# Attention's softmax sums inverted once per query, on 32 partitions, with GpSimd moving them through DRAM

## The chip, the cores and the metric

The kernel runs on one core of one Trainium2 chip. The metric is the device time of one launch in microseconds (us). TensorE is called PE here, VectorE DVE, ScalarE ACT, GpSimd POOL and SyncE SP, as in the rows of the profile.

## The reference, cut to what matters

The model is two layers of a transformer block with a mixture of experts. The change is in the attention alone. It has 1024 latent tokens and 256 context tokens, and 16 heads: eight with a low-rank key and value (MLA), eight with grouped queries (GQA). Latent queries read all 1280 keys; context queries, which only layer 0 has, read the 256 context keys.

```
s = jnp.einsum('bqhgd,bkhd->bhgqk', qblk, k, preferred_element_type=jnp.float32) * scale
p = jax.nn.softmax(s, axis=-1)
return jnp.einsum('bhgqk,bkhd->bqhgd', p.astype(v.dtype), v)
...
o = jnp.concatenate([blocked_attention(qm, [kmc, km], ...), blocked_attention(qg, [kgc, kg], ...)], axis=-1)
x = layer_norm(ALPHA * x + ga * (o @ w_o[l]), ln1_g[l], ln1_b[l])
```

The softmax divides by a sum over the keys, one sum for each query and head.

## The kernel before, in words

`attention` treats the 16 heads as 8 pairs. A unit `u` is a pair of heads with some tiles of 128 queries. A latent unit has 4 tiles (512 queries) and ten steps `k`, one for each tile of 128 keys; a context unit has 2 tiles (256 queries) and two steps. Layer 0 has, for each pair, a context unit, then a latent unit (called A here), then a latent unit (B): 24 units. Layer 1 has A and B alone, 16 units, and there each latent unit follows a latent unit. Pairs 0 to 3 are MLA, with six score matmuls a step; pairs 4 to 7 are GQA, with four.

In each step PE computes the scores of this step (`scores`, L1045), ACT takes the exponential (L1108), DVE adds it into an accumulator (`accumulate`, L1169), and PE multiplies it with the values (`values`, L1059; several steps at a time at k = 2, 5 and 8, the last two in the next unit's step 0). Beside this, each step prepares a coming unit: PE computes a whole row block of its scores (`begin`, L1015) and DVE takes the maximum of each query over it (`maximum`, L1155). The function `ahead` says which: steps 0 to 5 serve the next latent unit, steps 8 and 9 the one after, steps 6 and 7 none. At step 6 the maxima are turned (L1024), copied (L1128) and written by SP as a row of the queries (L950). All `begin` calls share one PSUM area `sc`, so a `begin` waits until the maximum before it is done.

After a unit's last values, in step 0 of the next unit, ACT copies the unnormalised output to `raw` (L1115). In step 1 PE sums the accumulator over the partitions by a matmul with ones (L1069): the sums of head 0 stand alike in partitions 0 to 63, those of head 1 alike in 64 to 127. ACT copies them to `den` (L1120). DVE inverts `den` into `rinv` in pieces of `RC` = 128 queries on all 128 partitions (`invert`, L1179): four pieces in steps 6 and 7 for a latent unit, two in steps 8 and 9 for a context unit. POOL multiplies `raw` by `rinv` (L1204), and SP stores the product (L956), all in the order of the units. `raw`, `den`, `rinv` and `ot` have two buffers each.

The order of each engine's instructions is the order of the code; nothing is reordered at run time. An instruction that waits holds all that stand behind it on its engine. POOL does nothing in the attention before but the 40 multiplications.

## Time and profile before

| | us |
|---|---|
| median of 3 runs | 4173.8 (4168.7 to 4178.05) |
| the profiled execution | 4167.26 |
| its span | 4165.5 |
| attention, layer 0, from the first maxima | 463 to 1116 |
| attention, layer 1 | 2567 to 3093 |
| busy: PE, DVE, ACT, POOL | 3411.0, 2815.2, 1832.2, 1344.3 |

The span is the time from the first to the last instruction. The busy shares (PE 82%, DVE 68%) are means over stages with different limits. What the change can do is read in the two attention stages, from what PE waits for there.

### The profile page before, as it was taken

How to read it: one execution, taken by the hardware profiler on the slowest of the kernel's cores; microseconds unless marked ns; L12 is line 12 of the kernel's file. 1: busy time of each engine (PE TensorE's matmuls, PEld its weight loads, DVE VectorE, ACT ScalarE, POOL GpSimd, SP SyncE). 2: the span in 40 equal slices, each digit the busy share in tenths (PEclk: the TensorE clock that was granted, in tenths of full speed). 3: DMA queues.
4: the chain of work that ended last, by engine and by line, in shares of the span. 5: the costliest groups of instructions: out<-in, count | busy, mean ns of one | idle time of the engine just before them, and what ended most of it. 6: DMA issues, size and time to landing. Idle time of an engine off the chain costs nothing. (4 is left out here: it accounts for less than half of the span.)

```text
span 4165.5 us, 44180 instructions
## 1 busy us (share of the span) xinstructions
PE 3411.0 (82%) x14128; PEld 2192.3 (53%) x14128; DVE 2815.2 (68%) x2943; ACT 1832.2 (44%) x2102; POOL 1344.3 (32%) x889
## 2 busy tenths in 40 slices
PE   5999598888588599999938994999868589999960
PEld 2554354544244488888814442554424368888850
DVE  1444366776455699899846663777854578989966
ACT  0222232333200388888823331333320068888850
POOL 2111000000100387777732210000010077777750
PEclk9999699998798699999969996999989789999985
DMA  7554621110222499688743326111022159797953
GB/s 291 198 204 158 160 50 45 44 33 24 107 87 89 193 396 355 265 317 321 305 181 120 125 95 176 47 50 41 16 93 86 67 234 383 307 361 298 354 226 115
DMA packets 247658, 730.56 MB, mean 175 GB/s; under 512 B 49232, under 2 KB 137072, under 8 KB 194184
## 3 DMA queue, kind: packets, MB, share of 16 engines
q0 software_dynamic: 104272, 508.74, 31.5%
q1 hardware_dynamic: 130328, 174.51, 13.6%
q10 hardware_dynamic: 12960, 46.15, 3.2%
q8 instruction: 44, 0.72, 0.1%
q14 instruction: 54, 0.44, 0.0%
HBM read 715.09 MB, written 129.34 MB: 203 GB/s over the span
## 5 line engine op out<-in xcount | busy, mean ns | idle before, releaser
L1879 DVE TENSOR_TENSOR ex_wl<-ex_wr,ex_wh 128x2048 fp32r<-128x2048 f32 x440 | 988.0, 2288 | 61.7 <-ACT ex_wh L1824 61.7
L1824 ACT ACTIVATE ex_wh<-ex_wr 128x2048 fp32r<-128x2048 f32 x440 | 842.7, 1915 | 73.7 <-PE ex_yp L1787 53.5
L1108 ACT ACTIVATE at_pt<-at_st 128x1024 f32<-128x1024 f32 (+1 forms) x336 | 336.6, 1004 | 652.4 <-PE at_st L1045 651.4
L1155 DVE TENSOR_REDUCE at_nm<-at_sc 128x1 f32<-128x1280 f32 (+1 forms) x276 | 376.7, 1365 | 254.6 <-PE at_sc L1015 252.3
L715 PE MATMUL zp<-w_in,hT 128*128 128x480 f32 x960 | 428.5, 580 | 24.8 <-ACT z L378 23.2
L1204 POOL TENSOR_TENSOR at_ot<-at_raw,at_rinv 128x512 f32<-128x512 f32 (+1 forms) x40 | 49.9, 1248 | 1229.7 <-DVE at_rinv L1179 1229.7
L1169 DVE TENSOR_TENSOR at_acc<-at_acc,at_pt 128x1024 f32<-128x1024 f32 x256 | 312.8, 1222 | 103.5 <-ACT at_pt L1108 102.2
L1367 PE MATMUL mr_mp<-mr_w_o,mr_oT 128*128 128x512 f32 x576 | 283.5, 655 | 100.8 <-DVE mr_bc L1435 40.9
L1059 PE MATMUL at_op<-at_pt,at_va 128*64 128x512 f32 (+1 forms) x1344 | 331.1, 623 | 0.2
L1705 POOL DMA_INDIRECT ex_wr<-in_w_down,piece_of x152 | 314.3, 2068 | 46.3 <-issue 46.3
L1045 PE MATMUL at_st<-at_q,at_km 96*128 96x512 f32 (+3 forms) x1008 | 272.4, 411 | 34.8 <-DMA at_q<-at_nmT 34.8
L715 PEld LDWEIGHTS zp<-w_in,hT 128*128 128x128 f32 x960 | 173.4, 194 | 172.8 <-issue 145.5
L1045 PEld LDWEIGHTS at_st<-at_q,at_km 96*128 96x128 f32 (+1 forms) x1008 | 183.8, 197 | 137.7 <-issue 55.3
L1367 PEld LDWEIGHTS mr_mp<-mr_w_o,mr_oT 128*128 128x128 f32 x576 | 119.6, 211 | 254.8 <-issue 190.8
L1764 PE MATMUL ex_gp<-ex_wh,ex_xh 128*128 128x512 f32 x576 | 226.7, 394 | 13.4 <-DVE ex_wl L1879 13.4
L1705 POOL DMA_INDIRECT ex_wr<-in_w_gate,piece_of x152 | 222.6, 1465 | 46.4 <-issue 46.4
L1782 PE MATMUL ex_yp<-ex_wh,ex_hh 128*128 128x512 f32 x576 | 233.2, 405 | 0.0
L1725 POOL DMA_INDIRECT y_s<-ex_y,row_to x72 | 193.0, 2680 | 118.6 <-ACT ex_y L1832 117.4
L1783 PE MATMUL ex_yp<-ex_wl,ex_hh 128*128 128x512 f32 x576 | 227.6, 395 | 0.0
L1765 PE MATMUL ex_gp<-ex_wl,ex_xh 128*128 128x512 f32 x576 | 226.1, 393 | 0.0
L1766 PE MATMUL ex_gp<-ex_wh,ex_xl 128*128 128x512 f32 x576 | 225.8, 392 | 0.0
L1766 PE MATMUL ex_vp<-ex_wh,ex_xl 128*128 128x512 f32 x576 | 224.5, 390 | 0.0
(266 smaller groups left out, 6003.9 us busy)
## 6 DMA issues: line engine op xcount, KB each, us to landing
ad_w<-in_w_ada POOLq DMA_DIRECT2D x48, 1024.0 KB, 10.6
q_mla<-qT SPq DMA_DIRECT2D x40, 384.0 KB, 3.9
k_mla<-kT SPq DMA_DIRECT2D x40, 384.0 KB, 5.8
at_km<-k_mla SPq DMA_DIRECT2D x16, 960.0 KB, 12.3
at_q<-q_mla SPq DMA_DIRECT2D x32, 384.0 KB, 12.6
w_in<-in_w_in SPq DMA_DIRECT2D x2, 5760.0 KB, 32.5
q_gqa<-gqT SPq DMA_DIRECT2D x20, 512.0 KB, 6.7
cy<-y_s POOLq DMA_DIRECT2D x10, 1024.0 KB, 5.2
```

What stands on the lines that cost most here:

```text
L715: ins = nc.tensor.matmul(zp[:, n, 0:ZW], hT[:, k, :], w_in[:, k, n * ZW:(n + 1) * ZW], start=(k == 0), stop=(k == KC - 1))
L1045: ins = nc.tensor.matmul(st[:, j % 2, h, 0:nq], kk, qq, start=(m == 0), stop=(m == len(passes) - 1))
L1059: ins = nc.tensor.matmul(op[VD * h:VD * h + VD, 0:nq], va[:, k, col * VD:(col + 1) * VD], pt[:, j % PT, h, 0:nq], start=(k == 0), stop=(k ...
L1108: nc.scalar.activation(pt[:, j % PT, :, 0:nq], st[:, j % 2, :, 0:nq], ACT.Exp).then_inc(exp_done, 1)
L1155: nc.vector.tensor_reduce(nm[:, v % 3, s:s + 1], score_bank(A_NO[v, s])[:, 0:kb * P], AX.X, ALU.max, negate=True).then_inc(max_done, 1)
L1169: nc.vector.tensor_tensor(out, before, pt[:, j % PT, :, 0:nq], ALU.add).then_inc(acc_done, 1)
L1367: ins = nc.tensor.matmul(mp[:, n * 512:(n + 1) * 512], oT[:, k, :], w_o[:, k, n * 512:(n + 1) * 512], start=(k == 0), stop=(k == KC - 1))
L1705: pool.indirect_dma_start(wr[:, u, p].rearrange("p a n -> p (a n)"), None, w, bass.IndirectOffsetOnAxis(R["wi"][:, p % 2, b:b + 1], 0), bo ...
L1766: ins = nc.tensor.matmul(out[:, :], xl[:, k, :], wh[:, q, j, :], start=False, stop=(k == KC - 1))
L1782: nc.tensor.matmul(out, hh[:, 2 * k + c, :], W[0][:, c, cols], start=(k == 0 and c == 0), stop=False)
L1824: nc.scalar.activation(wh[:, q], wr[:, u, p], ACT.Copy).then_inc(hi_done, 1)
L1879: nc.vector.tensor_tensor(wl[:, q], wr[:, u, p], wh[:, q].bitcast(F32), ALU.subtract).then_inc(lo_done, 1)
```

## The change

`RC` becomes 32. DVE no longer inverts the sums on 128 partitions, where 64 partitions hold the same numbers. POOL takes one row of each head (the rows that differ) from `den` to a DRAM buffer `den_s`, and from there to a tile `dc` in which 1024 sums stand as 32 partitions of 32 (512 sums as 16 of 32). DVE inverts that into `rc` in one instruction. POOL writes `rc` to DRAM (`inv_s`) and reads each head's inverses back into 64 partitions of `rinv`. Each transfer is waited for before the next that reads it. POOL does this for one unit after the other, and the unit's multiplication stands at the end of its chain. `inverted` says where DVE's instruction stands: after a latent unit in step 5, after a context unit in step 2 for the unit before it and in step 8 for the context unit itself. The last unit of a layer is not moved: DVE inverts its sums from PSUM in one instruction of 512 columns and multiplies itself; ACT's copy of them goes.

```diff
-    PT, QR, RC = 8, 5, P
+    PT, QR, RC = 8, 5, 32
+    def inverted(u, k):
+        if U[u][3] != NT or u == 0:
+            return []
+        if U[u - 1][3] == NT:
+            return [u - 1] if k == 5 else []
+        return [u - 2] if k == 2 and u > 1 else [u - 1] if k == 8 else []
...
-            take_sums(len(U) - 1)
...
-            def invert(u, pieces):
-                for i in pieces:
-                    if i == 0:
-                        dve.wait_ge(den_taken, u + 1)
-                        if u > 1:
-                            dve.wait_ge(ot_ready, u - 1)
-                    part = slice(i * RC, (i + 1) * RC)
-                    nc.vector.reciprocal(rinv[:, u % 2, part], den[:, u % 2, part]).then_inc(inv_done, 1)
+            def invert(u):
+                dve.wait_ge(dc_loaded, 16 * (u + 1))
+                n = 2 * U[u][2] * P // RC
+                nc.vector.reciprocal(rc[0:n, u % 2, :], dc[0:n, u % 2, :]).then_inc(inv_done, 1)
...
-                    if k in (6, 7):
-                        w = u - 2 if u and U[u - 1][3] != NT else u - 1
-                        if w >= 0:
-                            invert(w, range(2 * (k - 6), 2 * (k - 5)))
-                    if k in (8, 9) and u and U[u - 1][3] != NT:
-                        invert(u - 1, [k - 8])
-            invert(len(U) - 1, range(4))
+                    for w in inverted(u, k):
+                        invert(w)
+            u = len(U) - 1
+            nq = U[u][2] * P
+            dve.wait_ge(r_full, u + 1)
+            dve.wait_ge(ot_ready, u - 1)
+            nc.vector.reciprocal(rinv[:, u % 2, 0:nq], op[:, 0:nq]).then_inc(inv_done, 1)
+            dve.wait_ge(inv_done, u + 1)
+            dve.wait_ge(op_taken, u + 1)
+            dve.wait_ge(o_stored[u % 2], 16 * (u // 2))
+            dve.wait_ge(ot_ready, u)
+            nc.vector.tensor_tensor(ot[:, u % 2, ...], raw[:, u % 2, 0:nq], rinv[:, u % 2, 0:nq], ALU.mult)...
...
-            for u in range(len(U)):
-                nq = U[u][2] * P
-                pool.wait_ge(inv_done, pieces_done(u))
+            for u in range(len(U) - 1):
+                nq, s = U[u][2] * P, u % 2
+                n = 2 * nq // RC
+                pool.wait_ge(den_taken, u + 1)
+                for h in range(2):
+                    pool.dma_start(S["den_s"][s:s + 1, h * nq:(h + 1) * nq], den[VD * h:VD * h + 1, s, 0:nq])...
+                pool.wait_ge(den_kept, 32 * (u + 1))
+                pool.dma_start(dc[0:n, s, :], S["den_s"][s, 0:2 * nq].rearrange("(p b) -> p b", b=RC))...
+                pool.wait_ge(inv_done, u + 1)
+                pool.dma_start(S["inv_s"][s, 0:2 * nq].rearrange("(p b) -> p b", b=RC), rc[0:n, s, :])...
+                pool.wait_ge(r_kept, 16 * (u + 1))
+                if u >= 2:
+                    pool.wait_ge(ot_ready, u - 1)
+                for h in range(2):
+                    pool.dma_start(rinv[VD * h:VD * h + VD, s, 0:nq], S["inv_s"][s, h * nq:(h + 1) * nq].partition_broadcast(VD))...
+                pool.wait_ge(r_spread, 32 * (u + 1))
```

DVE, layer 0, from step 5 of unit A of the second pair to the context unit behind it, before (`at_nm` are the maxima, `at_acc` the accumulators, `at_den` the sums on 128 partitions):

```order
L1169 TENSOR_TENSOR at_acc<-at_acc,at_pt 128x1024 x2
L1179 RECIPROCAL at_rinv<-at_den 128x128 x2
L1169 TENSOR_TENSOR at_acc<-at_acc,at_pt 128x1024
L1179 RECIPROCAL at_rinv<-at_den 128x128 x2
L1155 TENSOR_REDUCE at_nm<-at_sc 128x1
L1169 TENSOR_TENSOR at_acc<-at_acc,at_pt 128x1024
L1179 RECIPROCAL at_rinv<-at_den 128x128
L1155 TENSOR_REDUCE at_nm<-at_sc 128x1
L1169 TENSOR_TENSOR at_acc<-at_acc,at_pt 128x1024
L1179 RECIPROCAL at_rinv<-at_den 128x128
```

The same engine and place in the changed kernel, from step 2 of that unit on (`at_dc` are the sums as 32 or 16 partitions of 32):

```order
L1175 TENSOR_TENSOR at_acc<-at_acc,at_pt 128x1024
L1181 RECIPROCAL at_rc<-at_dc 32x32
L1161 TENSOR_REDUCE at_nm<-at_sc 128x1
L1175 TENSOR_TENSOR at_acc<-at_acc,at_pt 128x1024
L1161 TENSOR_REDUCE at_nm<-at_sc 128x1
L1175 TENSOR_TENSOR at_acc<-at_acc,at_pt 128x1024
L1161 TENSOR_REDUCE at_nm<-at_sc 128x1
L1175 TENSOR_TENSOR at_acc<-at_acc,at_pt 128x1024 x3
L1161 TENSOR_REDUCE at_nm<-at_sc 128x1
L1175 TENSOR_TENSOR at_acc<-at_acc,at_pt 128x1024
L1181 RECIPROCAL at_rc<-at_dc 16x32
L1161 TENSOR_REDUCE at_nm<-at_sc 128x1
```

The four large inversions no longer stand between step 6 and the maximum of step 8; a small one stands behind step 2 and another behind step 8.

POOL, layer 0, a latent unit and the context unit behind it, before:

```order
L1204 TENSOR_TENSOR at_ot<-at_raw,at_rinv 128x512 x2
L1204 TENSOR_TENSOR at_ot<-at_raw,at_rinv 128x256
L1204 TENSOR_TENSOR at_ot<-at_raw,at_rinv 128x512 x2
L1204 TENSOR_TENSOR at_ot<-at_raw,at_rinv 128x256
L1204 TENSOR_TENSOR at_ot<-at_raw,at_rinv 128x512 x2
```

POOL in the changed kernel, one latent unit and the context unit behind it (`den_s` and `inv_s` are in DRAM):

```order
L1212 DMA den_s<-at_den 16x1x32 x2
L1214 DMA at_dc<-den_s 32x32
L1216 DMA inv_s<-at_rc 32x32
L1221 DMA at_rinv<-inv_s 64x512 x2
L1225 TENSOR_TENSOR at_ot<-at_raw,at_rinv 128x512
L1212 DMA den_s<-at_den 16x1x16 x2
L1214 DMA at_dc<-den_s 16x32
L1216 DMA inv_s<-at_rc 16x32
L1221 DMA at_rinv<-inv_s 64x256 x2
L1225 TENSOR_TENSOR at_ot<-at_raw,at_rinv 128x256
```

Each multiplication now has six transfers ahead of it, and the context unit's sums leave `den` only when the unit before it is multiplied.

## Rows read from the trace of the kernel before

**Rows 1.** Windows of the two attention stages: stretch, length, busy, clock, DMA.
```profile
463.00:1116.00 653.00, 536.72 (x2120) 295.46 (x2120) 436.63 (x392) 203.76 (x249) 35.02 (x36) 0.89 0.20 52
2567.00:3093.00 526.00, 465.55 (x1878) 252.61 (x1876) 391.65 (x328) 184.27 (x207) 21.76 (x16) 0.95 0.17 41
```

**Rows 2.** Waits of PE in these stretches: total us, times, longest.
```profile
PE at_sc L1015 <- DVE at_nm L1155: 68.1, 64, 1.8
...
PE at_sc L1015 <- DVE at_nm L1155: 30.6, 57, 1.4
```

**Rows 3.** Timeline of DVE, layer 1, GQA: start, us, instruction.
```profile
2901.30 1.76 DVE L1179 RECIPROCAL at_rinv<-at_den 128x128 f32<-128x128 f32 x2
...
2905.72 1.43 DVE L1155 TENSOR_REDUCE at_nm<-at_sc 128x1 f32<-128x1280 f32 x1
```

**Rows 4.** Timeline of PE: idle before and its releaser, in brackets.
```profile
698.26 0.84 PE L1015 MATMUL at_sc<-at_km,at_q 96*128 96x512 f32 x3 [1.10 <-DVE at_nm L1155]
...
917.30 0.84 PE L1015 MATMUL at_sc<-at_kg,at_q 128*128 128x512 f32 x3 [1.36 <-DVE at_nm L1155]
...
920.63 0.84 PE L1015 MATMUL at_sc<-at_kg,at_q 128*128 128x512 f32 x3 [1.54 <-DVE at_nm L1155]
...
2779.40 0.85 PE L1015 MATMUL at_sc<-at_km,at_q 96*128 96x512 f32 x3 [0.33 <-DVE at_nm L1155]
...
2907.20 0.86 PE L1015 MATMUL at_sc<-at_kg,at_q 128*128 128x512 f32 x3 [1.39 <-DVE at_nm L1155]
...
2922.08 0.85 PE L1015 MATMUL at_sc<-at_kg,at_q 128*128 128x512 f32 x3 [0.66 <-DVE at_nm L1155]
```

**Rows 5.** Groups of instructions, DVE, line 1179: count, busy, mean ns, idle before.
```profile
L1179 DVE RECIPROCAL at_rinv<-at_den 128x128 f32<-128x128 f32 x144 | 127.2, 922 | 3.6 <-ACT at_den L1120 3.6
```

**Rows 6.** Timeline, ACT's copies of sums, and DVE behind steps 2 and 5.
```profile
889.92 0.60 ACT L1120 ACTIVATE at_den<-at_op 128x512 f32<-128x512 f32 x1 [0.59 <-PE at_op L1069]
...
900.38 1.49 DVE L1155 TENSOR_REDUCE at_nm<-at_sc 128x1 f32<-128x1280 f32 x1 [0.87 <-PE at_sc L1015]
...
2915.24 0.60 ACT L1120 ACTIVATE at_den<-at_op 128x512 f32<-128x512 f32 x1 [0.58 <-PE at_op L1069]
...
2930.41 1.22 DVE L1169 TENSOR_TENSOR at_acc<-at_acc,at_pt 128x1024 f32<-128x1024 f32 x1 [2.18 <-ACT at_pt L1108]
```

**Rows 7.** Timeline of PE, last score matmul of step 9, unit A, GQA.
```profile
915.54 0.40 PE L1045 MATMUL at_st<-at_q,at_kl 65*128 65x512 f32 x1
```

**Rows 8.** Transfers by line: engine, count, KB each, median us from issue to landing.
```profile
cy<-y_s POOLq DMA_DIRECT2D x10, 1024.0 KB, 5.2
...
o_s<-at_ot SPq DMA_DIRECT2D x32, 256.0 KB, 2.5
...
mod<-ada POOLq DMA_DIRECT2D x4, 4.0 KB, 8.1
```

**Rows 9.** Line 1705, POOL's gathers of weights: issue to landing.
```profile
DMA to landing us min/median/max: 2.1/10.1/18.6
```

**Rows 10.** Line 1306, POOL: ns min/median/max of issuing a small transfer.
```profile
L1306 POOL DMA_DIRECT2D mr_b_r<-in_b_router_exp x2: 547/547/547, 1114.6 to 3102.2; - x2
```

**Rows 11.** DMA busy tenths in 40 slices of 886 to 926.
```profile
DMA  4999699200000000000000000000000071000047
```

**Rows 12.** Timeline, end of layer 1's attention; line 1401, a product of 128x512.
```profile
3087.92 0.60 ACT L1120 ACTIVATE at_den<-at_op 128x512 f32<-128x512 f32 x1 [2.20 <-PE at_op L1069]
3088.55 3.39 DVE L1179 RECIPROCAL at_rinv<-at_den 128x128 f32<-128x128 f32 x4 [1.81 <-ACT at_den L1120]
3092.02 1.26 POOL L1204 TENSOR_TENSOR at_ot<-at_raw,at_rinv 128x512 f32<-128x512 f32 x1 [6.36 <-DVE at_rinv L1179]
...
L1401 DVE TENSOR_TENSOR mr_u<-mr_mp,mr_bc x36: 680/692/693, 1149.0 to 3286.6; 128x512 f32<-128x512 f32 x36
```

**Rows 13.** Windows of two units of layer 1, GQA.
```profile
2905.88:2936.13 30.25, 26.70 (x109) 13.83 (x109) 24.99 (x22) 11.45 (x13) 1.26 (x1) 1.00 0.13 35
2936.13:2969.26 33.13, 29.54 (x109) 14.93 (x109) 25.08 (x22) 11.47 (x14) 1.26 (x1) 0.90 0.12 33
```

More of the change, by code:

```diff
@@ L897, in attention @@
         rinv = sb("rinv", [P, 2, 512])
+        dc = sb("dc", [2 * 512 // RC, 2, RC])
+        rc = sb("rc", [2 * 512 // RC, 2, RC])
         ot = sb("ot", [P, 2, 4, P])
@@ L908, in attention @@
         v_done, acc_done, op_taken = sem("v_done"), sem("acc_done"), sem("op_taken")
+        den_kept, dc_loaded, r_kept, r_spread = sem("den_kept"), sem("dc_loaded"), sem("r_kept"), sem("r_spread")
         r_full, den_taken, inv_done, ot_ready, o_stored = sem("r_full"), sem("den_taken"), sem("inv_done"), sem("ot_ready"), [sem(f"o_stored{s}") for s in range(2)]
@@ L914, in score_bank @@
             return st[:, :, :, :].rearrange("p b h n -> p (b h n)") if n < PRO and n % 2 else sc
-        def pieces_done(u):
-            return sum(unit[2] * P // RC for unit in U[:u + 1])
         def sums_done(u):
@@ new lines, in _ @@
+            nq = U[u][2] * P
[6 more added lines that the diff above has]
+            dve.wait_ge(ot_ready, u)
+            nc.vector.tensor_tensor(ot[:, u % 2, 0:U[u][2], :].rearrange("p a n -> p (a n)"), raw[:, u % 2, 0:nq],
+                                    rinv[:, u % 2, 0:nq], ALU.mult).then_inc(ot_ready, 1)
@@ L2018, in backbone @@
     dram("y_s", [NT * P * TOPK, D])
+    dram("den_s", [2, 2 * 512])
+    dram("inv_s", [2, 2 * 512])
     with ExitStack() as cx:
```

10 lines of the change are left out of this document (7 added, 3 removed).

## The prediction, made before the changed kernel ran

> **What bounds the kernel now.** I read the windows of the two attention stages first. They last 653 and 526 us, and PE is busy for 536.7 and 465.6 of them [rows 1], so PE is the engine to follow there: time that it does not wait is time won, as long as nothing else becomes late. The waits of PE come next. Its largest wait that recurs is that of the score block for a coming unit (L1015) for the maximum before it: 68.1 us in layer 0 and 30.6 us in layer 1 [rows 2]. That is the most that any relief of DVE could give back, 98.7 us; the question is which of these waits have an inversion ahead of them. The timelines of DVE and PE side by side tell. In a GQA unit of layer 1 two inversions stand behind step 6 and two behind step 7, and the maximum of step 8 starts only at 2905.72 [rows 3], though its scores were there some 4 us earlier; it ends at 2907.15, and PE, which has waited 1.39 us, starts the next block at 2907.20 [rows 4]. Where no inversion is near (steps 4 and 5), PE still waits 0.66 us [rows 4]: the step's four score matmuls are shorter than a maximum. That floor stays.
>
> **What goes.** DVE's 144 inversions of 128x128 take 127.2 us, 922 ns each [rows 5]. In their place stand 38 of 32 columns or fewer and two of 512. If the price goes by the columns (4 x 128 columns take 3.39 us in the end stage [rows 12], 6.6 ns a column), the small one costs 0.21 us, with a start of some tenths at most 0.4; 38 of them are 8 to 15 us of DVE. All of that has idle time of DVE behind it: 0.87 us after step 2 and 2.18 us after step 5 [rows 6]. I take its cost on the path as nothing; without that cover it would be at most 0.4 x 38 = 15 us. So DVE loses about 110 us of work, but little of it was on the path. By kind of unit (a wait and its floor; the row shown stands for its kind):
> - layer 1, GQA, B or A: the wait at step 9 is 1.36 to 1.39 in six units, 8.2 us in all; it goes. The wait one block later (0.75) falls to 0.66: 0.5 in all.
> - layer 1, MLA: 0.31 to 0.35 at step 9 in seven units, 2.3 us, goes; one block later 0.28 falls to 0.17 in six: 0.7.
> - layer 0, GQA, unit A, where the context unit's two inversions stand too: 1.36 and 1.54 us [rows 4], of which 0.66 stays: 2.25 each in three units, 6.7 us. The last pair has nothing to prepare.
> - layer 0, MLA, unit A: 0.33 and 1.10 [rows 4], of which 0.2 stays, three units: 3.7 us.
> - layer 0, GQA, unit B: 0.2 us, three times: 0.6. The waits of 1.6 to 1.8 us in these units, two blocks in a row with one maximum between, stay; they are most of layer 0's 68.1.
>
> Sum: 8.2 + 0.5 + 2.3 + 0.7 = 11.7 in layer 1 and 6.7 + 3.7 + 0.6 = 11.0 in layer 0.
>
> **The last unit.** Before: ACT's copy starts at 3087.92, the four inversions at 3088.55 take 3.39, POOL's product starts at 3092.02 and takes 1.26, end 3093.28 [rows 12]. After: DVE starts where ACT did, 3.4 us for 512 columns, then a product of 128x512 at 0.69 [rows 12]: 3087.92 + 3.4 + 0.07 + 0.69 = 3092.1. That is 1.2 us in each layer, 2.4 together, if POOL has finished the unit before it (below).
>
> **What comes in: 228 transfers on POOL's queue.** Six for each of 38 units. POOL itself is idle, and an issue costs it 0.55 us [rows 10]. What counts is the chain. Let H be the time from issue to landing of one. Sums to `dc`: 0.55 + 2H (two issues, a landing, a load). Inverses to `rinv` and the product: 2H + 0.55 + 1.27. No such transfer stands in this trace. From below: POOL's gathers landed in 2.1 us at best [rows 9]. From above: POOL's 4 KB ones in 8.1 us, in pieces of single numbers [rows 8]. Between: a store of 256 KB from SBUF to DRAM 2.5 us, and 1 MB by POOL 5.2 us [rows 8]. The nearest rows are the store and the fastest gather, so I take H = 2.3. Then `dc` is ready 5.2 us after the sums and the product ends 6.4 us after the inversion.
>
> The Trainium skill ("DMA: Bandwidth & Descriptors", section "Anatomy of one DMA") gives a transfer of this kind a fixed cost of about 2.0 us; by it the two chains would be 4.6 and 5.8 us, and the sum the same. No row here shows so small a transfer of POOL's alone.
>
> The windows these have to fit:
> - Step 5, layer 1: sums at 2915.24 + 0.60 = 2915.84, DVE needed again at 2930.41 [rows 6]: 14.6 us against 5.2. Free until H = 7.0.
> - Step 2, layer 0, GQA (the narrowest): sums at 890.52, DVE needed at 900.38 [rows 6]: 9.9 us against 5.2. Free until H = 4.6. The DMA engines are nine tenths busy up to 893 with query loads [rows 11], so H may be 1 or 2 us more for the first hop.
> - Step 8, layer 0: the context unit's sums can leave only after the unit before is multiplied. From the inversion at step 2 (about 899.6) POOL needs 2H + 1.8, then 0.55 + 2H: 4H + 2.4 = 11.6 us. DVE is needed for the maximum of step 9, whose block follows the scores of step 9 (last one at 915.54 + 0.28) by 0.75: about 916.6 [rows 7]. 17.0 us against 11.6. Free until H = 3.6. This is the tightest place.
> - Last unit: its steps are short, about 8.5 us from the sums to step 5 and 2.3 idle, 10.8 against 5.2; the product of the unit before ends about 9 us ahead of the end.
>
> SP waits for a product a little later or earlier than now, and its next loads are four units ahead of use. `raw` of a unit is overwritten two units later. Both are covered by more than 10 us.
>
> **Sum.** 11.0 + 11.7 + 2.4 = 25.1 us off the profiled execution's 4167.3: 4142. That execution was 6.5 us below the median of the runs shown, so in terms of that median 4173.8 - 25 = 4149.
>
> **Rivals.**
> 1. The clock pays too. Of two like units one took 30.25 us at a granted clock of 1.00 and the next 33.13 at 0.90 [rows 13]: stretches of 1.2 GHz cost 2.9 us there. Over layer 1 from step to step four such dips cost 6.7 us, in layer 0's GQA pairs and one MLA pair about 11. If fewer and shorter waits of PE kept the clock up, all of it might come on top: 25 + 14 = 39, 4135. For it: a dip followed waits. Against: the units before had the same waits and no dip, and the long waits of layer 0's B units stay.
> 2. The gain is eaten. Transfers under load take 4 to 4.5 us: step 8 is then late by 4 x 4.3 + 2.4 - 17.0 = 2.6 us in seven A units, 18 us, or the waits removed at step 9 return at the next block. About 4168.
> 3. Slower: the chain on POOL at step 8. Above H = 3.6 each further us of H costs 4 us in each of the seven A units of layer 0, because DVE stands still there with maxima behind it and PE behind those. Gain and loss balance at 25 / 28 = 0.9 more, H = 4.5; at H = 6 step 8 would be 9.4 us late and, with step 2 late by 2.7 already, the loss is 7 x 9.4 = 66 us, the time 4173.8 + 41 = 4215. For it: the 8.1 us row and the load at 886 to 893 [rows 8, 11]. Against: the engines are nearly idle for 17 of the 24 us after, and that row's 1024 pieces of 4 bytes are not like these 32 pieces of 128.
>
> The Trainium skill (the same page, "Latency and other measured facts") gives DRAM access 0.2 us on average and 2 us at high load. With 2 us more on the one hop that falls into the busy stretch, step 2 would need 7.2 of 9.9 us, and the sum stays; the rule counts against the change only if the load lasts, and [rows 11] show it ending at 893.
>
> 4. The change could miss its aim if the maximum of step 8 waited for something else. Its scores end some 4 us before it starts, and DVE is busy without a gap in between, so I give it nothing of its own.
>
> **Chances.** Forecast 0.62 (its own range 4141 to 4157), rival 1 0.14, rival 2 0.14, rival 3 0.10. What this kernel's measurement can tell from no change is about 0.2%, 8 us. Faster by more than that: the forecast, rival 1 and a fifth of rival 2, 0.77; within: 0.13; slower: 0.10. The range that should hold 8 in 10 is 4136 to 4170: the lower end cuts half of rival 1, the upper takes in rival 2 and leaves out rival 3.
>
> **What would show it.** Right: at step 9 PE's wait for L1155's line is gone in layer 1 and its GQA units take about 28.8 us instead of 30.25; DVE's small inversions take 0.2 to 0.4 us and DVE waits for no transfer ahead of them; the waits of 1.6 to 1.8 us in layer 0's B units are unchanged; after the sums the load of `dc` lands within 6 us; the end of the stage is a DVE product. Wrong: DVE idle ahead of the inversion at step 8 or 2 with a DMA as releaser (rival 3 or 2); waits at step 9 gone but as much added at the block after (rival 2); unit times shorter than 28.8 with a clock of 1.00 throughout (rival 1).

## The result and the profile after

| | median of n runs, us | kernel before in the same call | ratio, 95% interval |
|---|---|---|---|
| the changed kernel | 4127.56 (4121.3 to 4130.12), 4 | 4171.25, 4 | 0.9890 (0.9871 to 0.9908) |
| its profiled execution | 4127.45 | 4167.26 | |

The change took 43.7 us off by the medians and 39.9 us by the two profiled spans. The forecast was 25, which gave 4149 by the median that the prediction started from, with 4136 as the lower end of the range: the direction was right, the gain was forecast too small. Of the runs below, one execution of f4_idle_inv took 4876.61 us at a granted clock of 0.713; its times are read from the other three.

The two attention stages of the changed kernel, in the same columns as [rows 1]:

```profile
465.00:1092.00 627.00, 532.39 (x2120) 294.90 (x2120) 386.05 (x337) 203.16 (x248) 98.35 (x161) 0.90 0.23 59
2535.00:3053.00 518.00, 470.20 (x1904) 258.42 (x1903) 366.26 (x289) 183.97 (x207) 68.47 (x105) 0.95 0.22 59
```

DVE (the third of the busy times) is busy for 50.6 us less in layer 0. POOL (the fifth) went from 35.0 to 98.4 us there, for the issues. What PE waited for, in the changed kernel, first layer 0 and then layer 1, answers to [rows 2]:

```profile
PE at_sc L1022 <- DVE at_nm L1161: 58.5, 55, 1.9
...
PE at_sc L1022 <- DVE at_nm L1161: 18.7, 48, 0.8
```

9.6 us less in layer 0 and 11.9 us less in layer 1 (there the longest wait is now 0.8 us, not 1.4). Together 21.5 us: about half of the 39.9. The rest has to be found elsewhere. I cut both spans at ACT's copies to `raw`, of which each unit has one:

| us | before | after | less |
|---|---|---|---|
| start to the first copy | 504.3 | 507.1 | -2.7 |
| layer 0, units | 591.8 | 578.6 | 13.2 |
| its end (last copy to last product) | 8.1 | 5.9 | 2.2 |
| between the attention stages | 1520.2 | 1514.7 | 5.5 |
| layer 1, MLA units 1 to 7 | 224.4 | 219.6 | 4.8 |
| layer 1, GQA units 8 to 13 | 188.2 | 172.7 | 15.5 |
| layer 1, the last two units | 48.1 | 48.1 | 0.0 |
| its end | 8.2 | 5.9 | 2.2 |
| after it | 1072.2 | 1073.0 | -0.8 |

Of DVE in a GQA unit of layer 1 the timeline of the changed kernel reads as follows, where [rows 3] had two inversions of 1.76 us together and a late maximum:

```profile
2897.45 1.22 DVE L1175 TENSOR_TENSOR at_acc<-at_acc,at_pt 128x1024 f32<-128x1024 f32 x1
2898.58 0.33 DVE L1181 RECIPROCAL at_rc<-at_dc 32x32 f32<-32x32 f32 x1
2900.85 2.56 DVE L1175 TENSOR_TENSOR at_acc<-at_acc,at_pt 128x1024 f32<-128x1024 f32 x2 [1.93 <-ACT at_pt L1115]
2903.32 1.48 DVE L1161 TENSOR_REDUCE at_nm<-at_sc 128x1 f32<-128x1280 f32 x1
```

The small inversion costs 0.33 us and DVE is idle for 1.93 us behind it: it is hidden. The maximum of step 8 starts with no idle time and ends at 2904.80, ahead of PE, which starts the block of step 9 without a wait at 2906.37 and waits only at the block after it (timeline of PE, the changed kernel; the bracket is the idle time before):

```profile
2906.37 0.75 PE L1022 MATMUL at_sc<-at_kg,at_q 128*128 128x512 f32 x3
2907.14 0.50 PE L1052 MATMUL at_st<-at_q,at_kg 128*128 128x512 f32 x1
2907.48 0.39 PE L1052 MATMUL at_st<-at_q,at_kl 65*128 65x512 f32 x1
...
2908.70 0.85 PE L1022 MATMUL at_sc<-at_kg,at_q 128*128 128x512 f32 x3 [0.36 <-DVE at_nm L1161]
```

The chain on POOL for the same unit, each row with what POOL waited for:

```profile
2886.57 1.02 POOL L1212 DMA_DIRECT2D den_s<-at_den  x2 [9.14 <-ACT at_den L1127]
2888.93 0.51 POOL L1214 DMA_DIRECT2D at_dc<-den_s  x1 [1.33 <-DMA den_s<-at_den]
2899.21 0.51 POOL L1216 DMA_DIRECT2D inv_s<-at_rc  x1 [9.77 <-DVE at_rc L1181]
2901.08 1.04 POOL L1221 DMA_DIRECT2D at_rinv<-inv_s  x2 [1.37 <-DMA inv_s<-at_rc]
2904.73 2.35 POOL L1225 TENSOR_TENSOR at_ot<-at_raw,at_rinv 128x512 f32<-128x512 f32 x1 [2.61 <-DMA at_rinv<-inv_s]
```

A hop of this chain takes 1.6 or 1.7 us from issue to landing at the median (2.9 for the one that spreads a row over 64 partitions), and the sums are in `dc` some 4 us after the first issue. DVE waited for `dc` twice in the whole kernel:

```profile
DVE at_rc L1181 <- DMA at_dc<-den_s: 4.6, 2, 2.4
```

### The profile page after: what moved, and what is told of

It reads as the page before. It is cut to its first block and busy times, and to the rows that moved or that the text cites. A ratio compares the mean times of both kernels' runs of the same rounds, so it can differ in the third digit from the quotient of the medians.

```text
span 4125.6 us, 44304 instructions
## 1 busy us (share of the span) xinstructions
PE 3399.1 (82%) x14128; PEld 2189.6 (53%) x14128; DVE 2727.7 (66%) x2841; ACT 1830.7 (44%) x2100; POOL 1459.5 (35%) x1115
## 5 line engine op out<-in xcount | busy, mean ns | idle before, releaser
L1175 DVE TENSOR_TENSOR at_acc<-at_acc,at_pt 128x1024 f32<-128x1024 f32 x256 | 321.7, 1257 | 120.7 <-ACT at_pt L1115 118.5
L1785 PE MATMUL ex_vp<-ex_wh,ex_xh 128*128 128x512 f32 x576 | 224.1, 389 | 0.0
```

The source lines that it names most:

```text
L1175: nc.vector.tensor_tensor(out, before, pt[:, j % PT, :, 0:nq], ALU.add).then_inc(acc_done, 1)
L1785: nc.tensor.matmul(out[:, :], xh[:, k, :], wh[:, q, j, :], start=(k == 0), stop=False)
```

## The experiments

Twelve runs were made: of nine new kernels, and once more of the kernel before, of the changed one and of e3_xfer. In the comparison, "clean" means a unit that took its shortest time, in which TensorE was granted 2.4 GHz throughout; "half clock" is the time at 1.2 GHz in the clock record of the trace, counted from the span's start as the windows are. The table has the values on which the verdicts rest, in us. GQA and MLA are clean units of layer 1; "six" is the time of its GQA units 8 to 13 together. The runs were made in several calls, and the kernel before had medians from 4167.57 to 4181.37 in them, so whole times of different rows are compared by their ratios, each of which is against the kernel before in its own call.

| kernel | median | ratio, interval | layer 0 units, half clock | MLA | GQA | six, half clock |
|---|---|---|---|---|---|---|
| before (first profile) | 4171.25 | | 591.8, 89 | 32.05 | 30.24 | 188.2, 17 |
| f1_before2 | 4178.3 | 1.0005 (0.9983 to 1.0027) | 605.8, 126 | 32.05 | 30.24 | 183.4, 10 |
| e3_xfer | 4181.73 | 1.0025 (1.0007 to 1.0043) | 595.1, 96 | 32.05 | 30.24 | 185.9, 14 |
| f2_xfer2 | 4173.34 | 0.9991 (0.9971 to 1.0011) | 585.8, 70 | 32.05 | 30.25 | 184.7, 17 |
| f3_swap_before | 4136.87 | 0.9910 (0.9879 to 0.9941) | 562.8, 55 | 32.06 | 30.19 | 187.2, 14 |
| f4_idle_inv | 4130.7 | 0.9913 (0.9881 to 0.9945) | 571.6, 61 | 31.36 | 30.23 | 185.7, 14 |
| e2_moved | 4162.57 | 0.9972 (0.9955 to 0.9989) | 599.8, 102 | 31.36 | 29.05 | 174.3, 0 |
| e1_small | 4137.85 | 0.9911 (0.9881 to 0.9941) | 568.8, 58 | 31.35 | 28.52 | 172.8, 3 |
| after | 4127.56 | 0.9890 (0.9871 to 0.9908) | 578.6, 82 | 31.36 | 28.52 | 172.7, 3 |
| e4_after2 | 4127.47 | 0.9892 (0.9861 to 0.9923) | 572.6, 68 | 31.35 | 28.53 | 171.2, 0 |
| e6_noend | 4129.71 | 0.9907 (0.9876 to 0.9938) | 574.8, 72 | 31.36 | 28.52 | 172.8, 3 |
| e5_long | 4189.29 | 1.0045 (1.0023 to 1.0067) | 643.1, 147 | 31.4 | 28.5 | 173.6, 3 |
| e7_swap | 4097.62 | 0.9827 (0.9790 to 0.9864) | 547.8, 36 | 31.36 | 28.50 | 171.0, 0 |
| e8_mix | 4095.91 | 0.9831 (0.9794 to 0.9867) | 545.7, 44 | 31.36 | 28.52 | 171.2, 0 |

The first five rows have the long wait at step 9 of layer 1's GQA units by nature, the sixth has it put back, the other eight don't have it. The expectations below count the half clock by windows that lie 10.6 us too early in the clock record: where they say 97, 14, 7 to 14 and 0 to 3 us for rows of this table, it is 89, 17, 10 to 17 and 0 to 3, and their 324 between the attention stages is 320.

### e1_small: the DVE time of the inversions alone

```diff
                     part = slice(i * RC, (i + 1) * RC)
+                    part = slice(i * RC, i * RC + 8)
...
-                                        rinv[:, u % 2, 0:nq], ALU.mult).then_inc(ot_ready, 1)
+                                        den[:, u % 2, 0:nq], ALU.mult).then_inc(ot_ready, 1)
```

> The kernel before with each inversion cut from 128 to 8 columns and left in its place; POOL multiplies by the sums. Left out: 15 of 16 inversions, so the output is not the softmax's. Theory (only DVE's time ahead of the maximum of step 8 counts, and a wait of PE costs its idle time plus about 0.26 us of restart): units of layer 1 take 31.4 us (MLA) and 28.5 us (GQA), GQA unit A of layer 0 28.2 us, as in the changed kernel, and the whole some 40 us less than before, 4131 or a few less since no unit waits for a transfer and the end has no long inversion. Rival (the gain needs the new places of the instruction or the free ACT copy): units of 32.05 and 30.25 us stay, time within 10 us of before. Rival (only the idle time in the rows counts): gain of at most 30 us.

Measured: 4137.85 us. The attention has no transfer here and its layer 1 units are as short as in the changed kernel (31.35 and 28.52 us). So the gain inside the units is the DVE time taken off, and the transfers give nothing of it back there. The end stages are shorter (4.2 us each), which is the four inversions cut to 8 columns, and the stages behind the second attention take 1088 us in place of 1073. Since the values differ, the routing of the experts does too, so the whole time says nothing; only the units are read.

### e2_moved: the place alone

`inverted` is the changed kernel's.

```diff
-                    if k in (6, 7):
-                        w = u - 2 if u and U[u - 1][3] != NT else u - 1
-                        if w >= 0:
-                            invert(w, range(2 * (k - 6), 2 * (k - 5)))
-                    if k in (8, 9) and u and U[u - 1][3] != NT:
-                        invert(u - 1, [k - 8])
+                    for w in inverted(u, k):
+                        invert(w, range(U[w][2]))
```

> The kernel before with its 128x128 inversions, all of them, moved to the places of the changed kernel (step 5, or steps 2 and 8 after a context unit), no transfers. Theory: behind step 5 there are 2.2 us idle and slack up to the maximum of step 8, so layer 1 gains nearly all (units 31.4 and 28.5 us); behind step 2 there is only 0.9 us idle for 3.4 us of work, so GQA unit A of layer 0 takes about 31 us, no better than 30.7 before. Whole: about 4153. Rival (the amount of DVE work alone counts): no change, 4171. Rival (place alone counts): 4131 as in the changed kernel.

Measured: 4162.57 us. The full-size inversions at the new places are enough for MLA in layer 1 (31.36 us, all of the gain) and for two thirds of it in GQA. The timeline of PE around step 9 in this kernel shows why a third is missing:

```profile
2899.92 0.84 PE L1023 MATMUL at_sc<-at_kg,at_q 128*128 128x512 f32 x3 [0.17 <-DVE at_nm L1163]
2902.45 0.84 PE L1023 MATMUL at_sc<-at_kg,at_q 128*128 128x512 f32 x3 [0.74 <-DVE at_nm L1163]
```

The long wait fell to 0.17, but the next stayed at 0.74. In layer 0 four inversions do not fit behind step 2: in each of its A units with grouped queries PE waited 2.94 us there, and two of the three waited for maxima as long in all as before (4.35 and 4.42 us against 4.3); with 7 us of half clock in each they took 32.7 to 33.7 us. The layer's 8 us more than the first profile of before are within what two profiles of that kernel differ by. So the place gives most of layer 1's gain, and in layer 0 it gives none without the size: in e1_small, with the size alone, the A units with grouped queries took 28.20 to 28.23 us, as in the changed kernel. The whole time, 4162.57 us, lies some 10 us above the 4153 expected.

### e3_xfer and f2_xfer2: the transfers alone

The same kernel ran in two calls:

```diff
+                if u < len(U) - 1:
+                    n = 2 * nq // 32
+                    pool.wait_ge(den_taken, u + 1)
+                    for h in range(2):
+                        pool.dma_start(S["den_s"][s:s + 1, h * nq:(h + 1) * nq], den[VD * h:VD * h + 1, s, 0:nq])...
...
                 pool.wait_ge(inv_done, pieces_done(u))
+                if u < len(U) - 1:
+                    pool.dma_start(S["inv_s"][s, 0:2 * nq].rearrange("(p b) -> p b", b=32), dc[0:n, s, :])...
...
+                    for h in range(2):
+                        pool.dma_start(spread[VD * h:VD * h + VD, s, 0:nq], S["inv_s"][s, h * nq:(h + 1) * nq].partition_broadcast(VD))...
```

> The kernel before with POOL's six transfers a unit added, whose result nobody uses; DVE inverts on 128 partitions as before. Theory (transfers are hidden): units of 32.05, 30.25 and 30.7 us as before, time within 8 us of before, 4171. Rival (228 transfers cost through shared DMA engines or queues): slower by 10 us or more, with PE waits for at_q or at_km.

> The kernel before with all of the changed kernel's small transfers added, unused; the same as the run before of this kind. Theory (the transfers cost next to nothing in the attention and the 10 us of the medians were real but lie elsewhere, in how the experts' stages fall): a ratio of 1.002 to 1.003 again, units of 32.05 and 30.24 us at full clock as in the kernel before. Rival (the 10 us were scatter): a ratio of 0.999 to 1.001. A second rival (the transfers slow the attention's own steps): units longer than those of the kernel before by 0.2 us or more at full clock.

Measured: 1.0025 the first time and 0.9991 the second, with units of 32.05 and 30.24 us at full clock both times. The 228 transfers cost the attention nothing that can be seen. Behind the second attention both profiles took longer, 1079.4 and 1080.0 us against 1072.2 and 1073.5 in the two of the kernel before; e6_noend has 1078.3 too, and no run tells whether the transfers have a part in it. The 10 us of the first run did not come again: the interval of the first run leaves 1.000 out, that of the second holds it. A difference of this size had better be repeated before it is explained.

### e4_after2: the changed kernel again

> The changed kernel once more, for its time beside the others on one chip and for a second sample of the clock. Theory (some 5 us of the gain is the clock, which varies from run to run): about 4128 to 4135, unit times without a dip again 31.4, 28.5 and 28.2 us, dips in other places. Rival (the clock's part is fixed by the change): again a single dip in layer 1 between 2600 us and the stage's end.

Measured: 4127.47 us against 4127.56. In this profile no unit of layer 1 has a stretch of half clock.

### e5_long: a longer chain on POOL

```diff
+                for i in range(HOPS):
+                    pool.dma_start(dx[0:n, s, :], S["den_s"][s, 0:2 * nq].rearrange("(p b) -> p b", b=RC))...
+                    pool.wait_ge(x_loaded, 16 * (HOPS * u + i + 1))
```

(`HOPS` is 4; the loop stands ahead of the load of `dc`.)

> The changed kernel with four more loads, one after the other, ahead of each load of the 32 partitions: the sums reach DVE 4 x 1.9 = 7.5 us later. Theory: the windows are real. Layer 1 has 14.6 us and needs 4.4 + 7.5 = 12, so its units stay 31.4 and 28.5 us. In layer 0 DVE stands still behind step 2 for about 5 us in GQA unit A, and about 2 us behind step 8: some 50 us more than the changed kernel, 4178, which is slower than the kernel before. Rival (DVE's waits there are made up later): under 15 us more than the changed kernel. Rival (a hop costs PE everywhere): layer 1 slows as well.

Measured: 4189.29 us, some 60 above the changed kernel (59.6 above e6_noend in the same call) and 1.0045 of the one before. Layer 1's units did not change. In layer 0 DVE stood still, in order of time (timeline of DVE, this kernel):

```profile
859.01 0.34 DVE L1184 RECIPROCAL at_rc<-at_dc 32x32 f32<-32x32 f32 x1 [5.71 <-DMA at_dc<-den_s]
879.63 0.34 DVE L1184 RECIPROCAL at_rc<-at_dc 16x32 f32<-16x32 f32 x1 [4.65 <-DMA at_dc<-den_s]
```

and PE's waits for maxima went from 58.5 to 101.3 us, half clock in layer 0's units from 82 to 147. So the rival that ended slower is a real mechanism, at the places that the prediction named (steps 2 and 8 of the A units of layer 0); with hops of 1.6 to 2.9 us at the median the changed kernel is on the safe side of it.

### e6_noend: the end as before

```diff
-            dve.wait_ge(r_full, u + 1)
+            dve.wait_ge(den_taken, u + 1)
...
-            nc.vector.reciprocal(rinv[:, u % 2, 0:nq], op[:, 0:nq]).then_inc(inv_done, 1)
...
-            nc.vector.tensor_tensor(ot[:, u % 2, 0:U[u][2], :]...
+            for i in range(4):
+                part = slice(i * P, (i + 1) * P)
+                nc.vector.reciprocal(rinv[:, u % 2, part], den[:, u % 2, part]).then_inc(inv_done, 1)
...
+            nc.gpsimd.tensor_tensor(ot[:, u % 2, 0:4, :]...
```

> The changed kernel with the last unit of each layer as before: ACT copies the sums, DVE inverts four pieces, POOL multiplies. Theory (the end gained 2.2 us a layer, of which 1.0 is that DVE no longer has inversions ahead of its last additions): from ACT's copy of the values to the end 7.1 us instead of 5.9 (and 8.1 before), so 2.4 us more in all; by the total not to be told from the changed kernel, 4130. Rival (all 2.2 us are the shorter end): 8.1 us as before.

Measured: the segment from the last copy to the last product takes 7.22 us here, 5.94 in the changed kernel and 8.12 to 8.16 before. The shorter path of the last unit is worth 1.28 us a layer, as forecast (1.2). Another 0.9 us a layer comes from something else, told below.

### e7_swap, e8_mix and f3_swap_before: the waits that stayed

In layer 0's B units the score blocks of the coming latent and context unit stand in turn, and PE waits 1.6 to 1.8 us at several of them. e7_swap puts the context block first and takes both maxima into one turn:

```diff
-            return [(LATENT[n + 1], k + 2)] + ([(u + 1, k - 2)] if k >= 2 and U[u + 1][3] == CT else [])
+            return ([(u + 1, k - 2)] if k >= 2 and U[u + 1][3] == CT else []) + [(LATENT[n + 1], k + 2)]
...
-                pe.wait_ge(max_done, A_NO[v, 2 * na - 1] + 1)
+                w = v + 1 if v and U[v][3] == CT else v
+                pe.wait_ge(max_done, A_NO[w, 2 * U[w][2] - 1] + 1)
```

e8_mix has the second edit too, and moves two of the four context blocks into step 7 of the A unit:

```diff
+            return ([(u + 1, k - 2)] if k >= 4 and U[u + 1][3] == CT else []) + [(LATENT[n + 1], k + 2)]
+        if k == 7 and u + 2 < len(U) and U[u + 2][3] == CT:
+            return [(u + 2, 0), (u + 2, 1)]
```

> The changed kernel with the order of the two score blocks turned in layer 0's B units: the context unit's small block (maximum 0.42 us) first, the latent unit's (1.49 us) second; the turn waits for both maxima. Theory (long waits of PE for a maximum cost their time and pull the clock down): the four waits of 1.6 to 1.8 us a unit become about 0.6 us, B units are 4 us shorter in 7 pairs, and fewer dips of the clock follow: 28 to 40 us less than the changed kernel, about 4095. Rival (the waits move to the next block, behind the latent maximum): no gain beyond 8 us, since the next step's first block then waits for that maximum.

> As the swapped one, but two of the context unit's four blocks are made in step 7 of unit A, which is free since no inversion stands there any more. Theory: only two double steps are left in B units; gain over the changed kernel 28 to 40 us, some us more than the swap alone if step 7 has room. Rival (step 7 of unit A is full): A units grow by what B units lose.

f3_swap_before is the edit of e7_swap on the kernel before, inversions and all.

> The kernel before, with its large inversions left, and the order of two maxima changed: in layer 0's B units the score block of the coming context unit goes ahead of the latent one, and the wait of the step covers both maxima. In the changed kernel this took about 30 us off. Theory (this gain needs nothing of the inversions, it lies in steps 2 to 7 of the B units, where DVE has room in both kernels): 4171 - 30 = 4141, a ratio of 0.993, layer 0's units from 592 to about 562 us. Rival (it needs the DVE time that the inversions take, because in the kernel before two of them stand in each of the steps 6 and 7): half of it or less, 4155 to 4165, a ratio of 0.996 to 0.998, and the waits of PE at steps 7 to 9 of the B units grow from 0.7 to 1.5 us or more.

Measured: 4097.62, 4095.91 and 4136.87 us. The two orders cannot be told apart by their times: in e8_mix the A units with grouped queries grew from 28.2 to 29.9 and 31.4 us, and the B units behind them shrank from 34.3 to 34.9 us down to 32.3, so that the rival of that run describes it better than its theory. The swap takes 32 us off e6_noend in the same call, and by the ratio 38 us (25 to 51) off the kernel before: it needs nothing of the change. The two gains add within the noise: 0.9890 x 0.9910 is 0.980, and 0.9827 (0.9790 to 0.9864) was measured. The windows of layer 0's units, first of the changed kernel, then of e7_swap, tell how much of it is clock:

```profile
507.05:1085.65 578.60, 508.70 (x2051) 279.58 (x2051) 364.26 (x320) 198.52 (x241) 98.35 (x161) 0.93 0.17 46
```

```profile
505.41:1053.19 547.78, 496.98 (x2051) 271.35 (x2051) 361.02 (x319) 198.40 (x241) 98.20 (x161) 0.97 0.18 48
```

Half clock fell from 82 to 36 us. The same 2051 matmuls are busy for 11.7 us less, at a mean clock of 0.97 instead of 0.93; PE's waits for maxima fall from 58.5 to 39.2, 19.3 us. Their sum, 31.0, is the gain of the stretch (30.8).

### f1_before2 and f4_idle_inv: does the wait at step 9 pull the clock down?

f1_before2 is the kernel before, unchanged. f4_idle_inv is the changed kernel with the DVE work of before put back in layer 1's GQA units, its result unused:

```diff
+                    if len(U) == 16 and 8 <= u <= 14 and k in (6, 7):
+                        for i in range(2 * (k - 6), 2 * (k - 5)):
+                            nc.vector.reciprocal(spare[:, i * P:(i + 1) * P], den[:, (u - 1) % 2, i * P:(i + 1) * P])
```

> The kernel before, unchanged, once more, for its clock. Both theories expect the same time, 4165 to 4178 us, and the same waits at full clock: 1.36 to 1.39 us at step 9 of the units with grouped queries in layer 1, units of 30.2 us. They part on the half clock (1.2 GHz) in the six units 8 to 13 of layer 1. Theory (the long waits at step 9 let the clock fall): again some 14 us of half clock there, at least 8, and over 100 us in layer 0's units and the stages between taken as 97 and 324. Rival (the dips fall where they fall, and before and the kernel with added transfers were unlucky): 0 to 3 us as in the eight kernels without those waits.

> The changed kernel with four unused inversions of 128x128 put back behind steps 6 and 7 of the units with grouped queries of layer 1 (units 8 to 14), where the kernel before had its own; nothing else. All theories expect the wait at step 9 to come back at 1.36 to 1.39 us. Theory (a wait of PE costs its idle time and some 0.26 us of restart, and waits of this length let the clock fall): units 8 to 13 at full clock 30.24 us again instead of 28.52, and half clock of 7 to 14 us in them instead of 0 to 3; 171.1 + 6 x 1.72 + 3 to 7 = 184 to 188 us for the six, the whole kernel about 4127 + 13 = 4140. Rival A (a removed wait is worth its idle time alone, 1.45 us with the block after): 29.97 us, 180 to 181 us for the six. Rival B (the clock there has nothing to do with this wait): 30.24 us a unit but half clock of 0 to 3 us, 181 to 183 us for the six.

Measured in f4_idle_inv: the wait is back, and so are the unit of 30.23 us and the half clock, 14 us in the six units. The whole time does not show it: 4130.7 us where 4140 was expected, against 4127.5 for the changed kernel in other calls, by ratios that overlap. PE's wait, timeline of this kernel:

```profile
2912.34 0.84 PE L1023 MATMUL at_sc<-at_kg,at_q 128*128 128x512 f32 x3 [1.38 <-DVE at_nm L1162]
2914.86 0.84 PE L1023 MATMUL at_sc<-at_kg,at_q 128*128 128x512 f32 x3 [0.75 <-DVE at_nm L1162]
```

The windows of the six units, one fence each for before, after and f4_idle_inv (the last three numbers are clock, DMA share and GB/s):

```profile
2848.84:3037.01 188.17, 167.42 (x655) 86.14 (x656) 150.37 (x126) 68.84 (x79) 7.58 (x6) 0.95 0.08 22
```

```profile
2825.89:2998.60 172.71, 161.52 (x655) 83.97 (x656) 136.57 (x108) 68.87 (x78) 28.26 (x42) 0.99 0.12 33
```

```profile
2823.94:3009.59 185.65, 165.49 (x655) 85.79 (x656) 151.80 (x132) 68.80 (x78) 26.19 (x42) 0.96 0.11 31
```

655 matmuls each, with a clock of 0.95, 0.99 and 0.96. Over fourteen profiles the half clock of these units is 17, 10, 14, 17, 14 and 14 us in the six with the wait and 0, 3, 3, 0, 3, 3, 0 and 0 in the eight without it, in the order of the table: no overlap. The places of the dips say the same. The six profiles have 21 of them in these units, and 20 begin 0.2 to 2.8 us after the start of a block that had waited 1.36 to 1.39 us. One of them, behind the block that started at 2972.8 in f4_idle_inv, with the stretch after it (windows, the clock is the third number from the end):

```profile
2973.40:2976.70 3.30, 3.30 (x9) 1.99 (x7) 3.02 (x3) 1.02 (x1) 0.00 (x0) 0.50 0.00 0
2976.80:2980.20 3.40, 3.40 (x15) 1.65 (x15) 1.49 (x1) 0.95 (x2) 0.00 (x0) 1.00 0.00 0
```

The other rival would be that DVE's inversions bring the dips by themselves and not through PE's wait. e2_moved speaks against it: there DVE does the same work in these units (154.9 us busy, 150.4 before), the wait at step 9 is 0.17 us, and the clock never falls:

```profile
2847.00:3021.30 174.30, 160.01 (x657) 83.00 (x655) 154.94 (x126) 68.87 (x78) 12.73 (x6) 1.00 0.09 23
```

So the rival that the dips fall by chance is out; that a wait there brings them is shown by taking it away and by putting it back, the latter in one profile. How strongly they come is a matter of chance all the same: f1_before2 had 10 us where the first profile had 17 (its expectation asked for at least 8 in its own count, by which it is 7). And it is not the only thing that brings them: of the four dips in the eight profiles without the wait, three stand behind a wait of 0.75 us in step 5 and one behind a wait of 1.60 us for a row of maxima.

The other half of that expectation holds too: the units are 30.23 us, not the 29.97 of the rival that counts idle time alone. Where the 0.26 us lie is read from start to start, in the row above and in the changed kernel's rows ahead of the experiments. With the wait the two blocks start 2.52 us apart (2912.34, 2914.86), without it 2.33 (2906.37, 2908.70): 0.2 less, where the forecast had 0.09 (0.75 to 0.66). And counted from ACT's copy to `raw`, the first block starts 24.94 us into the unit with the wait and 23.43 without it, 1.5 us for a bracket of 1.38. The rows are from a clean unit of f4_idle_inv and from the changed kernel, where 2906.37 stands above:

```profile
2917.62 0.60 ACT L1123 ACTIVATE at_raw<-at_op 128x512 f32<-128x512 f32 x1 [2.45 <-PE at_op L1067]
2942.56 0.84 PE L1023 MATMUL at_sc<-at_kg,at_q 128*128 128x512 f32 x3 [1.38 <-DVE at_nm L1162]
```

```profile
2882.94 0.60 ACT L1122 ACTIVATE at_raw<-at_op 128x512 f32<-128x512 f32 x1 [2.11 <-PE at_op L1066]
```

## Why the prediction was wrong in size

Point by point, in the order of its working:

- **PE is the engine to follow, its waits for maxima the prize.** Right. In each clean unit the time follows PE's waits. The waits of 1.6 to 1.8 us in the B units stayed, as forecast.
- **The waits of layer 1.** Forecast 11.7 us, measured 6 x 1.73 + 7 x 0.69 = 15.2. Every wait went that was to go. One step failed here: taking a wait's price from its bracket, and the next one's floor from a bracket elsewhere. In GQA the two parts are 1.5 and 0.2 us, where the brackets had 1.36 and 0.09. The floor of 0.66 was itself well read: at step 4 of a unit of the changed kernel the blocks are 2.33 us apart, as they now are at step 9.

```profile
2861.66 0.75 PE L1022 MATMUL at_sc<-at_kg,at_q 128*128 128x512 f32 x3
...
2863.99 0.85 PE L1022 MATMUL at_sc<-at_kg,at_q 128*128 128x512 f32 x3 [0.66 <-DVE at_nm L1161]
```

  But at step 9 the same 2.33 us show a bracket of 0.36, since PE's first matmul behind the block starts 0.77 us after it there and takes 0.50, against 0.58 and 0.39 at step 4, and 2.52 us show 0.75. A bracket depends on how fast PE ran ahead of it; the distance between two starts does not. In MLA it is the same, 0.69 us against 0.44 by brackets (timeline of PE, first before, then the changed kernel):

```profile
2681.24 1.68 PE L1045 MATMUL at_st<-at_q,at_km 97*128 97x512 f32 x6
2683.24 0.85 PE L1015 MATMUL at_sc<-at_km,at_q 96*128 96x512 f32 x3 [0.33 <-DVE at_nm L1155]
2683.93 1.57 PE L1045 MATMUL at_st<-at_q,at_km 97*128 97x512 f32 x6
```

```profile
2662.44 1.67 PE L1052 MATMUL at_st<-at_q,at_km 97*128 97x512 f32 x6
2663.95 0.74 PE L1022 MATMUL at_sc<-at_km,at_q 96*128 96x512 f32 x3
2664.52 1.57 PE L1052 MATMUL at_st<-at_q,at_km 97*128 97x512 f32 x6
```

  From the matmuls ahead of the block to those behind it it is 2683.93 - 2681.24 = 2.69 us with a wait of 0.33 and 2.08 without: 0.61 us. The block itself takes 0.11 us longer after a wait, and it starts 0.16 later than the bracket alone explains.
- **The waits of layer 0.** Forecast 11.0. By the brackets A units gave 2.55 (GQA, three) and 1.22 (MLA, three), with the small ones of the B units 11.8 us, but two units kept a wait that was to go, 2.2 us (next point): 9.6, what the sums of PE's waits show. The MLA units gave 0.27 each on top (the one that kept no wait went from 32.44 to 30.96 us, 1.48 for 1.22), but the GQA units gave just their brackets (30.74 to 28.20, 2.54 for 2.55); no run tells why they differ. Right in size.
- **The small inversion, 0.2 to 0.4 us, hidden.** Right: 332 to 341 ns, 38 times, and the 16x32 ones took as long as the 32x32 ones.
- **Transfers: H = 2.3 and free below 3.6.** Right as a bound, with one exception. The first chain took some 4 us where 5.2 were forecast; the second, from DVE's inversion to the end of the product, took 7.0 to 8.2 where 6.4 were, for the spread takes 2.9 us and the product up to 2.35. First hops beside loads took 4.4 to 4.6 us in layer 0's GQA units and up to 6.1 in layer 1, within the windows. In layer 0's second and third A unit the first hop fell into the load of the next keys and queries:

```profile
666.06 1.03 POOL L1212 DMA_DIRECT2D den_s<-at_den  x2 [11.87 <-ACT at_den L1127]
675.64 0.51 POOL L1214 DMA_DIRECT2D at_dc<-den_s  x1 [8.55 <-DMA den_s<-at_den]
678.94 0.51 POOL L1216 DMA_DIRECT2D inv_s<-at_rc  x1 [2.80 <-DVE at_rc L1181]
```

  The second of its two transfers landed 8.8 us after its issue, DVE stood still for 2.43 us and PE for 1.39 instead of 0.17. The prediction had looked at the DMA load of one GQA unit only [rows 11]. The Trainium skill ("DMA: Bandwidth & Descriptors", section "Latency and other measured facts") gives 2 us of DRAM access at high load; the 8.8 us here are 7 above an undisturbed hop, and the measurement decides. For an undisturbed hop the same page's 2.0 us (section "Anatomy of one DMA") stands against 1.6 or 1.7 here.
- **The last unit.** Forecast 1.2 us a layer, measured 2.2. The edit itself gave 1.28 (e6_noend). The other 0.9 is a collision that the prediction had not seen. Timelines of the kernel before, of POOL, DVE and PE:

```profile
3083.54 2.12 POOL L1204 TENSOR_TENSOR at_ot<-at_raw,at_rinv 128x512 f32<-128x512 f32 x1 [20.78 <-DVE at_rinv L1179]
...
3083.38 3.36 DVE L1169 TENSOR_TENSOR at_acc<-at_acc,at_pt 128x1024 f32<-128x1024 f32 x2
...
3086.80 1.08 PE L1069 MATMUL at_op<-at_acc,c_ones 128*64 128x512 f32 x4 [1.72 <-DVE at_acc L1169]
```

  POOL's product of the last unit but one takes 2.12 us instead of 1.26, DVE's two additions beside it 3.36 instead of 2.49, and PE's sums wait 1.72 us for them. In e3_xfer and f2_xfer2 the product comes some microseconds later, the additions take 2.49 and the end is 7.24 to 7.29 us with all four inversions in it: 0.9 less, without the edit. In the changed kernel the product is over in time and PE's sums wait 0.79 us, for ACT. The Trainium skill ("SBUF — State Buffer", section "Who interferes with whom") says that GpSimd's ports are shared with the second pair of VectorE's and that this is an exclusive lock; the trace agrees. Taken singly, the first addition (3083.38) takes its usual 1.16 us and ends 1.0 us after the product began, which takes 0.86 longer than 1.26; the second (3084.65) takes 2.10 and ends 1.1 after the product. Each seems to stand still while the one that came first is at work. Where it happens in the middle of the changed kernel's units (2.35 us at 2904.73 above) nothing waits for it.
- **Rival 1, the clock, got 0.14.** This is the step of the forecast that failed most: the sum had nothing for the clock. It priced every removed wait at full clock, and held against rival 1 that the units before a dip had had the same waits and no dip. f4_idle_inv shows that a repeated wait of 1.4 us does bring dips, though not in each unit: that the unit before had the wait and no dip was no argument. In the six GQA units that was worth 188.17 - 6 x 30.24 = 6.7 us before and 1.6 after: 5.1 us. In layer 0's units PE was busy for 4.2 us less (512.85 against 508.70 for the same 2051 matmuls), and there were 7 us less of half clock (82 against 89), which account for 3.5 us at most (a dip of 3.4 us made a unit 0.7 or 1.6 us longer: 30.90 for 30.24 in f1_before2, 30.11 for 28.52 in the changed kernel).

The sum again, by measured terms: waits of layer 1 15.2 (forecast 11.7), layer 0 9.6 and 4.2 less of busy PE, of which part is clock (11.0), ends 4.4 (2.4), clock in layer 1's GQA units 5.1 (none). That is 38.5 us inside the attention, against 37.9 by the table of segments. The forecast's 25.1 lacks 3.5 us of waits in layer 1, 8.6 of clock (5.1 and 3.5) and 2.0 of the ends, and it had 0.7 too much in layer 0, where the late `dc` cost 2.2. The working of rival 1 came to 39 us, near to the 39.9 measured, and that is luck in part: it had 14 us for the clock in the attention, where 8.6 were found, and its own two terms, 6.7 and 11, make 17.7 and so 43 us. Its sign, units shorter than 28.8 us at a clock of 1.00 throughout, came true (28.52), but by the waits' price, not by the clock. The chances have a small slip too: 0.62, 0.14 and a fifth of 0.14 make 0.79, not 0.77.

**What stays open.** The stretch between the two attention stages is 5.5 us shorter in the changed kernel and has 9 us less of half clock (311 against 320). Over the fourteen profiles it is 1517 to 1522 us in the five kernels that wait at step 9 by nature and 1513 to 1520 in the others, so the scatter covers most of it. Nothing of the change stands there, and no run tells whether the shorter stage before it has a part in this. Layer 0's half clock scatters more: 89 and 126 us in two profiles of the same kernel. Part of it can be given to the change. The three A units with grouped queries, where waits of 1.36 and 1.54 us went, had 10, 19, 6, 6 and 9 us of half clock in the five kernels that have these waits, and none in the six profiles in which they are gone and nothing longer came (after, e1_small, e4_after2, e6_noend, e7_swap, f4_idle_inv). The B units, whose waits stayed, have most of the rest in both kernels (76 us before, 79 after), and there the single profiles decide. The pair of profiles shows a small gain for layer 0: its units took 594.6 us in the mean of the four profiles without change to its order (before, f1_before2, e3_xfer, f2_xfer2; 585.8 to 605.8) and 574.4 in the mean of four with the changed kernel's layer 0 (after, e4_after2, e6_noend, f4_idle_inv; 571.6 to 578.6), 20 us and not 13.

## What to carry to other kernels

A wait of the bounding engine can be worth more than its idle bracket (here in layer 1, not in layer 0's GQA units): price it from start to start of the instructions around it, against a place where it is absent. A recurring wait of over 1 us is priced at both clock levels, and the dearer one gets a real chance. Look at the DMA load of every kind of unit before trusting a slack for a small transfer. The largest waits deserve the first look, also where a change does not touch them: the swap of two blocks gave another 30 us or so in either kernel.

## What the runs showed of the hardware

- An inversion on DVE costs by its columns, not by its partitions: 194 ns for 128x8 (e1_small), 333 ns for 32x32 and 16x32 alike, 922 ns for 128x128, 3.36 us for 128x512 out of PSUM. The same 1024 distinct numbers cost 0.33 us as 32 partitions of 32 and 3.4 to 3.7 us as 128 partitions of 512.
- A small transfer on POOL's queue costs 0.51 us of POOL and lands in 1.6 or 1.7 us at the median, but in 8.8 us at worst beside large loads in the changed kernel.
- TensorE's granted clock fell to 1.2 GHz for 3.4 or 6.8 us right behind a wait of PE of 1.36 to 1.39 us, in 20 of 21 dips, though not behind each such wait.
- Two profiles of one kernel differed by 14 us in layer 0's units (591.8 and 605.8) by the clock alone; clean units agreed within 0.02 us. For a small change the clean unit is the sharper measure.
